# TensorE instead of GpSimd for three sums of squares, and a tile copied ahead of a split

## The reference

```python
h = rmsnorm(x, norm_mix_pre[layer])
y = mix_even(h, ...) if layer % 2 == 0 else mix_odd(h, ...)   # ends in "@ w_out"
x = x + rmsnorm(y, norm_mix_post[layer])
h = rmsnorm(x, norm_ffn_pre[layer])
f = (silu(h @ w_gate) * (h @ w_up)) @ w_down
x = x + rmsnorm(f, norm_ffn_post[layer])
```

## Time and profile before

| | |
|---|---|
| median of 3 runs | 1869.71 us (1869.35 to 1870.46) |
| the profiled execution's own time | 1875.0 us |
| its span, first to last instruction | 1873.2 us |
| PE busy | 1743.0 us (93%), 13272 instructions |
| DVE busy | 1191.5 us (64%) |
| ACT busy | 835.9 us (45%) |
| POOL busy | 259.3 us (14%), 243 instructions |
| mean granted TensorE clock | 0.960 |

### The profile page before, as it was taken

The page is one execution under the profiler, slowest core; times in us unless marked ns, Lnnn a source line. Parts: engine busy times, 40 slices in busy tenths (PEclk is TensorE's granted clock), DMA queues, the critical chain, the costliest instruction groups (busy, mean ns, idle before and its releaser), DMA issues.

```text
span 1873.2 us, 32546 instructions
## 1 busy us (share of the span) xinstructions
PE 1743.0 (93%) x13272; PEld 1666.2 (89%) x13272; DVE 1191.5 (64%) x1630; ACT 835.9 (45%) x1117; POOL 259.3 (14%) x243
## 2 busy tenths in 40 slices
PE   7999998899999999998899996998999987789998
PEld 6999997689999999998699995987999986579997
DVE  5555585785556755594785645566766586467664
ACT  5333463363335333463453433664434356443333
POOL 0002300210032002400130032221100012320000
PEclk9999998999999999999999998997999998689999
DMA  6455442135544455443154552343355432035552
GB/s 215 176 179 186 160 180 90 68 135 179 183 181 152 157 178 184 162 171 122 45 193 157 194 203 96 117 143 113 125 190 207 174 121 95 23 113 180 181 206 84
DMA packets 37814, 281.94 MB, mean 151 GB/s; under 512 B 4368, under 2 KB 4496, under 8 KB 7136
## 3 DMA queue, kind: packets, MB, share of 16 engines
q1 hardware_dynamic: 36016, 271.73, 40.8%
q0 software_dynamic: 1712, 9.02, 1.4%
HBM read 279.69 MB, written 1.05 MB: 150 GB/s over the span
## 4 chain that ended last, share of the span: by engine, by line
PE 76%; DVE 11%; ACT 8%; issue 3%; POOL 1%; DMA 1%; SPq 0%; DVEq 0%; ACTq 0%; POOLq 0%
PE bank L641 23%; PE bank L643 23%; PE bank L642 23%; DVE w_lo L1884 4%; ACT w_hi L1284 4%; ACT h L1348 1%; ACT h_hi L1347 1%; PE bank L959 1%; PE bank L1053 1%; DVE o_rstd L2393 1%; PE bank L1079 1%; PE bank L1066 1%; POOL h L577 1%; DMA raw<-in_up_w 0%; PE bank L996 0%
## 5 line engine op out<-in xcount | busy, mean ns | idle before, releaser
L1884 DVE TENSOR_TENSOR w_lo<-raw,w_hi 128x2048 fp32r<-128x2048 f32 (+3 forms) x238 | 580.9, 2441 | 294.0 <-ACT w_hi L1284 293.6
L641 PE MATMUL bank<-h_hi,w_hi 128*128 128x272 f32 (+1 forms) x2336 | 674.8, 289 | 35.4 <-DVE w_lo L1884 20.9
L643 PE MATMUL bank<-h_hi,w_lo 128*128 128x272 f32 (+1 forms) x2336 | 671.4, 287 | 0.0
L642 PE MATMUL bank<-h_lo,w_hi 128*128 128x272 f32 (+1 forms) x2336 | 671.1, 287 | 0.0
L1284 ACT ACTIVATE w_hi<-raw 128x2048 fp32r<-128x2048 f32 (+2 forms) x241 | 481.1, 1997 | 299.0 <-PE bank L643 295.8
L641 PEld LDWEIGHTS bank<-h_hi,w_hi 128*128 128x128 f32 x2336 | 446.8, 191 | 42.9 <-issue 27.6
L643 PEld LDWEIGHTS bank<-h_hi,w_lo 128*128 128x128 f32 x2336 | 446.7, 191 | 0.0
L642 PEld LDWEIGHTS bank<-h_lo,w_hi 128*128 128x128 f32 x2336 | 445.5, 191 | 0.1
L641 PE MATMUL bank<-g_hi,w_hi 128*128 128x256 f32 (+1 forms) x1344 | 390.5, 291 | 15.0 <-DVE y L1912 5.3
L643 PE MATMUL bank<-g_hi,w_lo 128*128 128x256 f32 (+1 forms) x1344 | 385.0, 286 | 0.0
L642 PE MATMUL bank<-g_lo,w_hi 128*128 128x256 f32 (+1 forms) x1344 | 384.0, 286 | 0.0
(11 more groups left out here) (339 smaller groups left out, 1882.4 us busy)
## 6 DMA issues: line engine op xcount, KB each, us to landing
raw<-in_up_w SPq DMA_DIRECT2D x131, 1024.0 KB, 4.9
raw<-in_down_w SPq DMA_DIRECT2D x48, 1408.0 KB, 5.9
raw<-in_in_w SPq DMA_DIRECT2D x20, 1024.0 KB, 4.9
raw<-in_out_w SPq DMA_DIRECT2D x16, 1024.0 KB, 4.9
raw<-in_even_w SPq DMA_DIRECT2D x12, 1024.0 KB, 4.9
raw<-in_odd_w SPq DMA_DIRECT2D x6, 1024.0 KB, 4.9
diag<-in_conv_w POOLq DMA_DIRECT2D x4, 1024.0 KB, 5.1
raw<-in_in_w SPq DMA_DIRECT2D x4, 512.0 KB, 3.6
```

Source lines behind the costliest of these rows:

```text
L641: pe.matmul(out, w[0], x[0], start=first, stop=False)
L642: pe.matmul(out, w[0], x[1], start=False, stop=False)
L643: return pe.matmul(out, w[1], x[0], start=False, stop=last)
L1884: dve.tensor_tensor(lo[:, 0:n], raw[:, slot, 0:n], hi[:, 0:n].bitcast(F32), ALU.subtract)\
```

## The change

GpSimd no longer adds the squares of a new residual in any of the three places; `second_sum` on TensorE now waits for each of the eight squares and accumulates eight products with the ones in bank 7. And in the last chunk of a mixer's output projection (second block only) VectorE copies tile 6 before it splits the coming chunk, where it did it after.

```diff
 # GpSimd
             for units in (range(UN), range(UN, 3 * UN)):
                 if units[0]:
-                    add_tiles(squared, sq, S, KD)
+                    seen.skip(squared, KD)
                 else:
                     seen.skip(squared, KD)
                 divide(units)
                 add_tiles(squared, sq, S)
-                add_tiles(squared, sq, S, KD)
+                seen.skip(squared, KD)
                 add_tiles(squared, sq, S)
 # TensorE
             def second_sum():
-                pe.wait_ge(acc_ready, seen.next(acc_ready))
-                pe.matmul(ps[7][:, 0:S], ones[:], acc[:, 0:S], start=True, stop=True).then_inc(var_ready, 1)
-                seen.skip(squared, KD)
+                for k in range(KD):
+                    pe.wait_ge(squared, seen.next(squared))
+                    last = pe.matmul(ps[7][:, 0:S], ones[:], sq[:, k, 0:S], start=k == 0, stop=k == KD - 1)
+                last.then_inc(var_ready, 1)
 # VectorE
             def project_out(n=T, l=None, restore=False):
                 for c in range(OUT_CHUNKS):
-                    if c:
+                    if c and (n == T or c + 1 < OUT_CHUNKS):
                         split_next(2 * KD if c + 1 < OUT_CHUNKS else UP_BLOCKS, 0, c + 1)
...
                             copy_tile(bass.ds(2 * c + e, 1), ps[4 + e])
+                            if c + 1 == OUT_CHUNKS:
+                                split_next(UP_BLOCKS, 0, c + 1)
```

## The result

The changed kernel takes 1879.51 us (median of 20 runs, 1872.5 to 1882.0) against 1870.39 us for the kernel before in the same sessions (20 runs, 1865.9 to 1876.2). The ratio is 1.0041, with a 95% interval of 1.0030 to 1.0052: 7.7 us slower, between 5.6 and 9.7 (the medians lie 9.1 apart, the means of the 20 runs 7.8). Forecast were 7.1 us more. The profiled execution has a span of 1878.2 us, 5.0 more than before's.

A forecast was written before the change was run, and what follows sets the result against it. TensorE was taken as the bound, with 76% of the chain. Added products cost 9.0 us, the copy gains 1.95: 7.1 us more on the timed median 1869.71 gives 1876.8 us, range 1873.3 to 1880.0.

The forecast's parts named there:

- The price of a product: In each sum on TensorE, one f32 product with the ones was to take 0.43 us between starts.
- The upper end, 0.76 us: Cost of one sum product if its two 378 ns records ran end to end; 16 us over three places.
- The chain from the sum to the fourth chunk: After each sum, its end starts work that TensorE awaits; a later sum delays the fourth chunk equally, TensorE's wait unchanged.
- Part 1: Sum of squares on TensorE: seven added products in each of three places, 3.0 us each, 9.0 us slower.
- The relief at nothing: VectorE up to 3.2 us earlier per place without GpSimd's additions, priced at nothing because TensorE's products cover it.
- the cover of 0.37 us: Second place, sixth tile: h_lo is written 0.37 us before TensorE comes to it, the tightest point.
- Part 2: Tile 6's copy ahead of the split in two mixers' output projections: 0.15 and 1.8 us, 1.95 us gained.
- Both guesses about the loads: For wx_hi in the mixers: first load stays late, gaining 0.15 us; second takes the usual time, gaining 1.8 us.
- The clock: TensorE's slow stretches after waits, left out of the sum; a 3 us stretch at half clock costs 1.5 us.
- Rival C: Second place's wait also followed by a slow clock stretch, 1.5 us more: 1878.3 to 1879.6 us; chance 0.12.
- nothing later takes the 3.0 us back: After each sum, the 3.0 us delay stays: TensorE is the bound behind each place and its loads move along.

The follow-up runs named there:

- sum twice: Changed kernel with the eight products of each sum made twice over; ratio 1.0085 to the kernel before, 15.9 us slower.
- early sum with copy: Kernel before with TensorE's one sum product moved ahead of the third chunk and tile 6 copied before the split; ratios 0.9942 and 0.9940 to before.
- copy only: Kernel before with only VectorE's copy of tile 6 put ahead of the split; ratio 0.9990, 1.9 us faster.
- sum only: Kernel before with only the sum of squares moved to TensorE, VectorE's order unchanged; ratio 1.0055, 10.3 us slower.
- adds kept: Changed kernel with GpSimd's 21 additions still running, result unused, TensorE waiting for the last; ratio 1.0033 to the kernel before, 6.2 us slower.

## Why the prediction was right, step by step

- **The price of a product**, 0.43 us: 3.45 us for eight in the trace of after. The upper end, 0.76 us, was wrong.
- **The chain from the sum to the fourth chunk**: 5.12 to 5.22 us in every kernel with the sum in its old place, and TensorE's waits unchanged in after, with the sum on TensorE alone and with the sum twice. Moving the sum brought them to 0.3 us, none and 0.5 us, which shows the cause rather than a coincidence.
- **Part 1, 9.0 us**: 10.3 (8.0 to 12.5) alone by the runs; in the profile of after 2.83, 3.02 and 3.16 us, 9.0 together. That the three add up so well is in part luck, since slow stretches of the clock within the pairs move each by some tenths (with the sum alone it is 2.64, 3.02 and 2.72 us).
- **The relief at nothing**: the cover of 0.37 us held. VectorE ended the third chunk's split 2.9 to 3.0 us earlier in each place, counted from the pair's first product, and idled; with the additions kept the second pair was the same.
- **Part 2, 1.95 us**: the profile of after shows 0.18 and 1.75 us (forecast 0.15 and 1.8), 1.93 together. Both guesses about the loads held: the even mixer's stayed late, the odd mixer's came on time because the longer sums moved the fetch. That makes the gain of the copy a gift of part 1: alone it was worth 0.73 us in its profile. And of the odd mixer's 1.75 us, 0.5 isn't the copy's: it is the product of tile 7's square, whose two records took 1.22 us at the slow clock before and 0.70 after, and 0.70 as well with the sum on TensorE alone. The copy's own share was 0.18 and 1.22 us, 1.40 in place of 1.95, so the agreement of the whole is luck.
- **The clock.** Rival C's mechanism came: the second place's wait was followed by a slow stretch, as the other two. The row of 1527 to 1530 us in the earlier trace rows ends before TensorE goes on at 1530.25; the first row below is the one behind that wait, before, and bears the reading out. Then TensorE's stretches after the three waits, after:

```profile
1530.00:1532.00 2.00, 1.75 (x15) 1.78 (x16) 1.97 (x7) 0.00 (x0) 0.00 (x0) 1.00 0.47 98
...
1334.00:1336.00 2.00, 2.00 (x10) 2.00 (x11) 2.00 (x3) 1.24 (x3) 0.00 (x0) 0.50 0.47 127
1535.00:1537.00 2.00, 1.75 (x8) 1.78 (x9) 1.97 (x7) 0.00 (x0) 0.00 (x0) 0.53 0.46 74
1692.00:1694.00 2.00, 2.00 (x13) 2.00 (x12) 2.00 (x2) 1.13 (x3) 0.00 (x0) 0.53 0.64 160
```

These stretches lie behind the intervals that I summed, so they aren't in the 7.1. Yet the whole span grew by 5.0 us only, and the mean granted clock over the span rose from 0.960 to 0.963. The profiles show where the 2.1 us left over lie, in two stretches of 0.8 and 1.5 us, with 0.2 us the other way elsewhere. Ahead of the even mixer's split, where nothing was changed in any kernel, the two differ by 0.8 us (1297.46 and 1296.68). That part takes 1292.9 to 1300.4 us in the twelve profiles, and 1300.35 and 1294.55 in the two of the same kernel (early sum with copy), so it says nothing of the change. The 1.5 us lie between the second place's dev and the odd mixer's split by ScalarE, in the same work, 674 records of TensorE's products before as after (us, the engines' busy time as in the earlier trace rows, granted clock):

```profile
1525.03:1651.34 126.31, 99.47 (x674) 84.86 (x674) 77.56 (x161) 66.57 (x168) 28.49 (x36) 0.84 0.22 74
...
1530.03:1654.87 124.84, 97.45 (x674) 84.58 (x673) 77.80 (x161) 66.65 (x168) 28.31 (x36) 0.86 0.22 73
```

This stretch takes 126.3 us in the two profiles with one product at the old place (before, copy only), and 124.3 to 124.8 us in the three with eight (after, sum only, adds kept). So the prediction's sentence that nothing later takes the 3.0 us back doesn't hold in these profiles: some 1.5 us come back as a higher granted clock, 0.86 instead of 0.84, although the second place's wait is now followed by a slow stretch. It isn't shown why, nor that it is so in every execution, since each of these kernels was profiled once; sum twice has 127.3 us.

The time lies 7.7 us above before by the ratio where 7.1 was forecast: the price of the products and the path that they lie on were right. The absolute time was closer to a miss: 1879.51 us, 2.7 above the forecast 1876.8 and 0.5 below the upper end of the range. The forecast's own weak point was the base: three runs of before lay within 1.1 us of each other, twenty within 10.2 us.

## What to carry to other kernels

Before a reduction is moved from a slow engine to the one that bounds, look whether anything waits for the slow one. Here it was 5.1 to 6.2 us early, so the move could only cost its own work, and each product cost in full since a chain to the bound engine's next chunk hung on the last one. What paid was the order: the same sum 24 products earlier, with the other engine's result, took nearly all of the wait away. The kernel before became 9.9 and 12.7 us faster in two measurements, the changed one 10.5 us.

## What the runs showed of the hardware

- An f32 product of 128x256 with ones is two records of 378 ns, and takes 0.43 us of TensorE at full clock from start to start, against 0.12 us for an f32r matmul of the same shape: 3.6 times, and not twice, as two passes at the f32r price would be.
- A 1 MB load whose transfer meets a fetch of TensorE's instructions 0.5 to 2.1 us before its end landed 0.8 to 1.6 us late in all but one such case of the table (0.5 us, lag 0.09); one fetch at 0.3 us went with a lag of 0.20. With fetches 6.8 us or more before there was no lag above 0.2 us. Inserting instructions that do nothing moved the fetch and shortened the mixer by 1.2 to 1.4 us.
- An h_lo of 128x256 takes 0.47 us alone and up to 1.01 us beside an addition on GpSimd, a split of 128x2048 2.29 and 2.84 us.
- After waits of TensorE of 2.4 to 2.8 us the granted clock mostly fell to 0.50, but not always. Of the six profiles with the sum in its old place all show it behind the first place's wait and five behind the third's. Behind the second's, of 2.5 us in all, it stayed at 1.00 in the two with one product (before, copy only) and fell in the four with eight or sixteen.
- The same instructions took 1292.9 to 1300.4 us up to the even mixer's split in twelve executions.
